# A hybrid attention and Hyena layer on one core: merge inputs read during the last inverse, m kept on chip, first tail weights split in the merge stage

## What is computed

```python
h = _rmsnorm(x, norm1_g) * (1.0 + scale1) + shift1
proj = h @ w_in
...
z = x1 * _fftconv(v, hf[:, 0], hy_bias[0])
return x2 * _fftconv(z, hf[:, 1], hy_bias[1])          # o_hy
...
g_attn, g_hy = jnp.split(jax.nn.sigmoid(gates), 2, axis=-1)
merged = g_attn * (o_attn @ w_br_attn) + g_hy * (o_hy @ w_br_hy)
x = x + gate1 * (merged @ w_out)
h2 = _rmsnorm(x, norm2_g) * (1.0 + scale2) + shift2
x = x + gate2 * (jnp.square(jax.nn.relu(h2 @ w_up)) @ w_down)
```

## Time and profile before

| | |
|---|---|
| Time, median of 3 runs | 2893.49 us (2892.32, 2893.49, 2897.98) |
| The profiled execution's own time | 2890.1 us |
| Its span | 2888.3 us |
| TensorE busy | 2707.6 us, 94% |
| VectorE, ScalarE, GpSimd busy | 44%, 31%, 28% |
| Mean granted TensorE clock | 0.961 of full speed |

### The profile page before, as it was taken

The page is one execution under the profiler, slowest core; times in us unless marked ns, Lnnn a source line. Parts: engine busy times, 40 slices in busy tenths (PEclk is TensorE's granted clock), DMA queues, the critical chain, the costliest instruction groups (busy, mean ns, idle before and its releaser), DMA issues. The chain is left out here.

```text
span 2888.3 us, 36192 instructions
## 1 busy us (share of the span) xinstructions
PE 2707.6 (94%) x14803; PEld 2318.0 (80%) x14803; DVE 1273.6 (44%) x1882; ACT 895.7 (31%) x1500; POOL 803.8 (28%) x551
## 2 busy tenths in 40 slices
PE   9687999999999999999898699798999999999998
PEld 7566887788888898888677588587888888888886
DVE  7566664445565445444876511326211212212215
ACT  2342221045555455554211421214122121121121
POOL 3546984111001010100233033213232232232230
PEclk9778999999999999999999799899999999999999
DMA  6666775442213221311756432501111111111101
GB/s 199 215 209 235 227 229 194 146 155 94 95 54 114 101 95 53 110 70 69 250 187 226 179 115 113 213 30 37 37 37 37 38 43 37 37 37 37 44 23 73
DMA packets 101858, 324.75 MB, mean 112 GB/s; under 512 B 12337, under 2 KB 30355, under 8 KB 101310
## 3 DMA queue, kind: packets, MB, share of 16 engines
q1 hardware_dynamic: 75678, 230.68, 23.2%
q0 software_dynamic: 26016, 91.76, 9.4%
HBM read 237.99 MB, written 76.02 MB: 109 GB/s over the span
## 5 line engine op out<-in xcount | busy, mean ns | idle before, releaser
L89 PE MATMUL tl_b<-tl_hi,tl_whi 128*128 128x512 f32 (+1 forms) x960 | 344.9, 359 | 21.2 <-DVE tl_lo L2447 15.3
L90 PE MATMUL tl_b<-tl_lo,tl_whi 128*128 128x512 f32 (+1 forms) x960 | 342.6, 357 | 0.0
L91 PE MATMUL tl_b<-tl_hi,tl_wlo 128*128 128x512 f32 (+1 forms) x960 | 341.7, 356 | 0.0
L2388 DVE SCALAR_TENSOR_TENSOR tl_x<-tl_b,all_mod,tl_x 128x512 f32<-128x512 f32 (+1 forms) x216 | 142.5, 661 | 375.1 <-PE tl_b L91 362.8
L2282 POOL TENSOR_TENSOR tl_wlo<-tl_raw,tl_whi 128x1024 fp32r<-128x1024 f32 x72 | 178.3, 2478 | 445.5 <-ACT tl_whi L2201 445.5
L89 PE MATMUL tl_b<-tl_uhi,tl_whi 128*128 128x512 f32 (+1 forms) x768 | 275.1, 358 | 3.5 <-POOL tl_ulo L2292 3.5
L91 PE MATMUL tl_b<-tl_uhi,tl_wlo 128*128 128x512 f32 (+1 forms) x768 | 276.6, 360 | 0.0
L89 PE MATMUL at_out<-h_hi,at_whi 128*128 128x424 f32 (+1 forms) x672 | 263.9, 393 | 12.8 <-POOL at_wlo L510 10.9
L90 PE MATMUL tl_b<-tl_ulo,tl_whi 128*128 128x512 f32 (+1 forms) x768 | 274.5, 357 | 0.0
L695 DVE TENSOR_REDUCE at_nmax<-at_s 128x1 f32<-128x1280 f32 (+1 forms) x160 | 196.8, 1272 | 111.9 <-PE at_s L562 111.3
L510 POOL TENSOR_TENSOR at_wlo<-at_raw,at_whi 128x1024 fp32r<-128x1024 f32 x28 | 66.2, 2363 | 626.5 <-ACT at_whi L611 626.5
(11 more groups left out here) (295 smaller groups left out, 5777.3 us busy)
## 6 DMA issues: line engine op xcount, KB each, us to landing
tl_raw<-in_w_tail SPq DMA_DIRECT2D x72, 512.0 KB, 3.7
hy_tab<-in_hy_tab POOLq DMA_DIRECT2D x68, 512.0 KB, 4.9
hd_wa<-in_w_adaT SPq DMA_DIRECT2D x32, 512.0 KB, 4.3
at_raw<-in_w_proj SPq DMA_DIRECT2D x28, 512.0 KB, 4.6
fd_in<-in_xT SPq DMA_DIRECT2D x16, 640.0 KB, 4.6
s_gatesT<-at_pad SPq DMA_DIRECT2D x16, 640.0 KB, 2.9
mg_gate<-s_gatesT SPq DMA_DIRECT2D x16, 640.0 KB, 5.0
fd_in<-in_w_ada SPq DMA_DIRECT2D x16, 512.0 KB, 4.0
```

What stands on the lines that cost most here:

```text
L89: pe.matmul(out, w_hi, x_hi, start=first, stop=False)
L90: pe.matmul(out, w_hi, x_lo, start=False, stop=False)
L91: return pe.matmul(out, w_lo, x_hi, start=False, stop=last)
L2388: dve.scalar_tensor_tensor(out=x1[:, n, at:at + m], in0=bank[x % GEMM_BANKS][:, 0:m], scalar=g.mod[:, gate, SEG_OF[c]:SEG_OF[c] + 1], in1= ...
```

## The change

The loads of x2 and of the first four heads of o move from the start of the merge stage into the Hyena stage, behind its last forward product, into the room of `e_hi` to `o_lo` (`early_at`). In the merge's first loop ScalarE now scales all ten units of heads 0 and 1, two behind each of the ten blocks, where ScalarE and VectorE had five each of every head behind the loop. GpSimd writes m into eight rows on chip (`m_row`), in places that are free by then; the stores, the loads and the DRAM tensor are gone. The tail's weight unit 0 is loaded, rounded and subtracted during the last merge unit. The tail reads `m_row` directly, and its x1 load follows the one of weight unit 1.

```diff
@@ stage_hyena
+        x2 = st.over("x2", early_at, [P, CHT, T])
+        o_first = st.over("o0", early_at + 4 * CHT * T, [P, ON_Z * UNITS, VD])
...
+            sp.wait_ge(runs, RUNS + FWD_RUNS)
+            sp.dma_start(x2[:], g.convT[2 * CHT:].rearrange("c p t -> p c t")).then_inc(early_in, 16)
+            for h in range(ON_Z):
+                sp.dma_start(o_first[:, h * UNITS:(h + 1) * UNITS], g.o[h]).then_inc(early_in, 16)
+            sp.wait_ge(early_in, 16 * (1 + ON_Z))
@@ stage_merge, sync
-            x2_from = g.convT[2 * CHT:].rearrange("c p t -> p c t")
-            for s, cols in enumerate((slice(CTX, T), slice(0, CTX))):
-                sp.dma_start(x2[:, :, cols], x2_from[:, :, cols]).then_inc(x_in[s], 16)
-            load_head(0)
             load_w(0, 0)
-            for h in range(1, ON_Z):
-                load_head(h)
...
-                sp.wait_ge(summed, NC * (n + 1))
-                sp.dma_start(g.mT[n], gate[s][:, 0]).then_inc(stored[s], 16)
                 if n + 2 < KD:
-                    sp.wait_ge(stored[s], 16 * (n // 2 + 1))
+                    sp.wait_ge(summed, NC * (n + 1))
                     load_gates(n + 2, s)
-            for s in range(2):
-                sp.wait_ge(stored[s], 16 * KD // 2)
+            sp.wait_ge(mm, NC * (KD - 1))
+            sp.dma_start(next_raw[:], g.d["w_tail"][0]).then_inc(next_in, 16)
@@ stage_merge, scalar
                 act.activation(o_hi[:, 0:CHT, block_columns(n)], oh[n % OH][:], ACT.Copy).then_inc(oh_h, 1)
-            act.wait_ge(small, 4)
-            scale_units(0)
+                if n == 0:
+                    act.wait_ge(small, 4)
+                for r in range(n * ALL_ACT, (n + 1) * ALL_ACT):
+                    ins = scale_unit(r // UNITS, r % UNITS)
+                    if r % UNITS == UNITS - 1:
+                        ins.then_inc(scaled_act, 1)
             weights(0)
             for h in range(HEADS):
-                if h + 1 < HEADS:
+                if ALL_ACT <= h + 1 < HEADS:
                     scale_units(h + 1)
                 upper(h)
...
+            act.wait_ge(next_in, 16)
+            act.activation(next_hi[:], next_raw[:], ACT.Copy).then_inc(next_split, 1)
@@ stage_merge, gpsimd
-                    pool.tensor_tensor(gt[:, 0, at:at + m], gt[:, 0, at:at + m], gt[:, 1, at:at + m], ALU.add
+                    if c == 0 and n in (KD - 3, KD - 2):
+                        pool.wait_ge(lo_done, n + 2)
+                    elif c == 0 and n == KD - 1:
+                        pool.wait_ge(summed, NC * n)
+                    pool.tensor_tensor(m_row[n][:, at:at + m], gt[:, 0, at:at + m], gt[:, 1, at:at + m], ALU.add
                                        ).then_inc(summed, 1)
+                    if (n, c) == (KD - 1, 1):
+                        pool.wait_ge(next_split, 1)
+                        pool.tensor_tensor(next_lo[:], next_raw[:], next_hi[:], ALU.subtract)
@@ stage_tail, sync and scalar
-            load(0)
-            for k in range(KD):
-                if k >= RAW:
-                    sp.wait_ge(m_l, k - RAW + 1)
-                sp.dma_start(m_raw[k % RAW][:], g.mT[k]).then_inc(m_in[k % RAW], 16)
-                if k == RAW - 1:
-                    load(1)
+            load(1)
             sp.dma_start(x1[:], g.d["xT"].rearrange("k p t -> p k t")).then_inc(x_in, 16)
...
-            weights(0)
             for k in range(KD):
-                act.wait_ge(m_in[k % RAW], 16 * (k // RAW + 1))
-                act.activation(hi[:, k], m_raw[k % RAW][:], ACT.Copy).then_inc(m_h, 1)
-                if k == RAW - 1:
+                act.activation(hi[:, k], m_row[k][:], ACT.Copy).then_inc(m_h, 1)
+                if k == KD // 2:
                     weights(1)
+            act.wait_ge(m_l, KD)
```

More of the change, by code:

```diff
@@ L1844, in stage_merge @@
         gate = [st.over(f"gate{s}", first_at + s * 8 * T, [P, 2, T]) for s in range(2)]
+        m_at = [z_at + 4 * T * k for k in range(4)] + [oh_at, raw0_at, x2_at, first_at]
+        m_row = [st.over(f"m{k}", at, [P, T]) for k, at in enumerate(m_at)]
+        next_at = raw0_at + 4 * T
+        next_hi, next_lo = (st.over(f"next{x}", next_at + i * 4 * KD * P, [P, KD, P], F32R) for i, x in
+                            enumerate(("hi", "lo")))
+        next_raw = st.over("nextraw", next_at + 8 * KD * P, [P, KD, P])
+        assert next_at + 12 * KD * P <= oh_at
         e2, var, std, scale = (st.sb(n, [P, N]) for n in ("e2", "var", "std", "scale"))
@@ L1848, in stage_merge @@
         oh_bank = bank[0] + bank[1][:1]
-        raw_in, gate_in, stored = ([st.sem(f"{n}{s}") for s in range(2)] for n in ("raw_in", "gate_in", "stored"))
-        o_in = [st.sem(f"o_in{h}") for h in range(HEADS)]
-        x_in = [st.sem(f"x_in{s}") for s in range(2)]
+        raw_in, gate_in = ([st.sem(f"{n}{s}") for s in range(2)] for n in ("raw_in", "gate_in"))
+        next_in, next_split = st.sem("next_in"), st.sem("next_split")
+        o_in = [st.sem(f"o_in{h}") for h in range(ON_Z, HEADS)]
         hi_done, lo_done, sig, mm, gated, summed = (
@@ L2130, in stage_tail, with weight_tile @@
     with stage(nc, "tl") as st:
+        def weight_tile(name, dt=F32R):
+            return st.sb(name, [P, KD, P], dt)
+        u_at = st.place()
+        assert u_at == from_at
+        u_hi, u_lo = (st.sb(x, [P, GT, T], F32R) for x in ("uhi", "ulo"))
+        r = [st.sb(f"r{s}", [P, 512]) for s in range(2)]
+        var, std, rstd = (st.sb(x, [P, 2, TT]) for x in ("var", "std", "rstd"))
+        st.sb("spare", [P, (rows_to - st.place()) // 4])
         x1 = st.sb("x1", [P, KD, T])
@@ L2133, in stage_tail @@
         hi, lo = (st.sb(x, [P, KD, T], F32R) for x in ("hi", "lo"))
-        raw = [st.sb(f"raw{s}", [P, KD, P]) for s in range(2)]
-        w_hi = [st.sb(f"whi{s}", [P, KD, P], F32R) for s in range(W_SLOTS)]
-        w_lo = [st.sb(f"wlo{s}", [P, KD, P], F32R) for s in range(W_SLOTS)]
-        r = [st.sb(f"r{s}", [P, 512]) for s in range(2)]
+        raw = [next_raw, weight_tile("raw1", F32)]
+        w_hi1, w_lo1, w_hi2, w_hi3 = (weight_tile(n) for n in ("whi1", "wlo1", "whi2", "whi3"))
+        assert st.place() == next_at
+        st.sb("next", [P, 3 * KD * P])
+        w_lo2, w_lo3 = (weight_tile(n) for n in ("wlo2", "wlo3"))
+        w_hi, w_lo = [next_hi, w_hi1, w_hi2, w_hi3], [next_lo, w_lo1, w_lo2, w_lo3]
         a = st.sb("a", [P, KD, 2])
-        var, std, rstd = (st.sb(x, [P, 2, TT]) for x in ("var", "std", "rstd"))
-        u_at = st.place()
-        u_hi, u_lo = (st.sb(x, [P, GT, T], F32R) for x in ("uhi", "ulo"))
         row = 4 * T
-        m_raw = [st.over(f"mraw{s}", u_at + s * row, [P, T]) for s in range(RAW)]
         sq = [st.over("sq", u_at, [P, 2, T]), st.over("fsq", hi_at, [P, 2, T])]
@@ L2151, in stage_tail @@
         raw_in = [st.sem(f"raw_in{s}") for s in range(2)]
-        m_in = [st.sem(f"m_in{s}") for s in range(RAW)]
         x_in, hi_done, lo_done, m_h, m_l, mm, added, relu, squared, u_h, u_l, a_done = (st.sem(x) for x in (
@@ L2318, in job @@
                 kind, unit, n, c = JOBS[x]
-                pe.wait_ge(lo_done, unit + 1)
+                pe.wait_ge(lo_done, unit)
                 free(x)
```

79 lines of the change are left out of this document (40 added, 39 removed).

## The result

| | before | after |
|---|---|---|
| Time, median | 2892.9 us (4 runs) | 2864.8 us (2869.85, 2855.16, 2866.71, 2862.89) |
| Ratio | | 0.9898, 95% interval 0.9882 to 0.9914 |
| The profiled execution, span | 2890.1 us, 2888.3 us | 2869.85 us, 2868.0 us |

The change makes the kernel faster by 1.0%: 28.1 us between the medians, 29.5 by the ratio. Two single executions of the study stand far apart (7756.1 us of the kernel before, 3843.49 us of the one with 672 bytes of padding); they are in the medians given and left out of the ratios.

A forecast was written before the change was run, and what follows sets the result against it. TensorE, busy 94% of the span, was taken as the bound, so its waits were counted: -7.9 - 8.7 - 7.6 + 1.3 = -22.9 us, from 2893.5 to 2870.6 us, range 2866 to 2874 (61%), wider 2865 to 2881.

The forecast's parts named there:

- Part 1: Head of the merge stage: no wait for x2, two groups of units off ScalarE's path, loop 1.1 longer; 7.9 us gained.
- Part 2: End of merge to tail: m stays on chip, so the path is barrier, rounding, split, product; 8.7 us gained.
- Part 3: Tail's first jobs: the residual lands before job 4 needs it, so 5.90 us of wait and the restart go; 7.6 us.
- the slow restart: Tail, after the gap at job 4: eight products took 3.52 us against 1.84 at full clock; 1.7 us to be gained.
- Part 4: Last inverse: the early loads share the DMA with a critical table, so TensorE resumes 1.3 us later.
- even halves: Last inverse: assumed that the two DMA queues share evenly, so the table's 0.5 MB take 2.6 us instead of 1.3.
- the upper bound of the forecast: Last inverse: all 5.24 MB of early loads served first, spectrum up to 13.0 us late; as a rival 16%, 2874 to 2882.3.
- they only write elsewhere: End of the merge: GpSimd's sums for m were taken to cost the same as before.
- more than forecast: Rival, 3%: a shorter restart at the tail's start and no cost of the early loads; 2864 to 2866 us.
- the clock did not stay low: Rival "slower", 3%: TensorE's clock could stay low through merge unit 0 after the earlier start; 2899 us and up.
- the residual landed at 1840.2: Rival, 8%: the residual still makes job 4 wait in the tail; 2878.2 if all is lost, else about 2873 to 2875.
- the twenty units did not pace the loop: Rival, 7%: the units pace the merge's first loop, 1.4 us a turn instead of 1.2, losing 2 us; 2872.6.

## Why the prediction was right, and where it was wrong

**Part 1 was right**: -7.9 forecast, -8.2 by stretch. The 6.2 us of the wait for x2 went, the two groups of units went (2.9), and the loop grew by 0.57 us, not by the 1.1 that I took. I had read VectorE's pace wrongly: 1.15 us a turn was the mean over a loop whose first two blocks come 0.6 apart, and the even pace is 1.20, in both kernels. ScalarE's 1.10 to 1.12 in its first turns fit into that, so only the two units of the last turn lengthen the loop. Undoing the twenty units cost 2.35 us, and undoing the early loads 7.1 by the profile: 5.5 for x2 (the first multiplication came 8.03 us behind the barrier and not 2.53), and 1.7 more because ScalarE's first turn then waited for head 0.

**Part 2 was right**: -8.7 forecast, -9.4 measured. From ScalarE's start on the first row to the product it took 2.85 us (it was 3.40), which is most of the difference; the barrier took the rest.

**Part 3 was right**: the wait of 5.9 us and the slow restart of 1.7 are gone, and the residual landed after 16.3 us (estimated 17). Holding the load back brought both back, the restart at the same 1.7. The row of -8.0 is near -7.6 partly by luck. From the tail's first product to job 4 it was 25.03 us and became 19.71, only 5.3 less, since the first products ran at a granted clock of 0.50 for longer (6.2 us against 4.6); and 1.0 us fell away behind job 4, most of it at a wait of the norm (3.4 us where it was 4.2), which I had not forecast. In the repeated kernel after, the first stretch is 18.28 (3.1 us at 0.50) and nothing falls away behind.

**Part 4 was right in kind and too small**: 1.3 forecast, 3.3 measured. The burst ended about where I had put it: SyncE's packets thin out from 1571.5 on, and its last data moved at 1574.68, which is 1563.2 counted as before (the last forward product came at 1554.90, 11.45 us later than in the earlier trace rows), against the 1559 to 1563 of the forecast. The step that was mis-sized is "even halves". The table had no packet moved for 3.8 us behind its issue, 2.6 us more than before, and shared only from then on, which cost the other half microsecond. Nor was the sharing even: in half microseconds from 1571.5, 13 packets of the table against 30 of SyncE's, then 21 against 27, 37 against 14, 49 against 12. The Trainium skill (DMA: Bandwidth & Descriptors, Queues, rings and completion order) has the engines go round the queues with work packet by packet. The trace shows no even halves; it doesn't refute the rule either, since a packet of the Trainium skill is a group of descriptors, and the profile's are single pieces of 4 or 5 KB.

A rival stands that the prediction did not name: service in the order of issue. The spectrum and the two tables that GpSimd had issued at 1553.86 and 1554.38, ahead of the burst, came in time; the critical table, issued behind it, got its first packet when 95% of the burst had moved. If the 16 engines finish such a queue one after another, the packets change over by degrees, as they do here. Late descriptors of the table would look alike. No run here tells these apart. What was not seen is the upper bound of the forecast, with all 5.24 MB ahead of the spectrum as well.

**The step that failed is a term that the sum does not have.** Of the moved rows I wrote "they only write elsewhere", and I costed the new layout of the tail at nothing. I never looked at the addresses. Between the first and the last DOWN product there are 848 us in which the diff changes only where things lie, and there it gained 8.9 us, since u_hi and u_lo came to lie a multiple of 256 bytes from the weights. With it the sum would have been -31.8 and the forecast 2861.7; the median measured is 3.1 us above that. The rival "more than forecast" named a shorter restart and a free part 4. The restart at the tail's start was 0.6 us longer in the profile after and 0.9 shorter in its repeat, and part 4 was not free. Its 2864 to 2866 also lie further below 2870.6 than the 1.3 us of part 4 and a restart of 1.7 can give. So its 3% and the range's low end of 2865 were too tight for want of the missing term.

None of the other rivals came true. The merge's products took 181.63 us where they took 182.03, so the clock did not stay low; the residual landed at 1840.2, 5 us ahead of its need; and the twenty units did not pace the loop.

## What to carry to other kernels

Where a diff allocates tiles anew, compare the time of a product in a stretch that the diff leaves alone before adding up its waits: 2.4% less for each product of 512 columns there was worth 8.9 us, as much as each of the three parts that were aimed at. Lay float32 operands of 512 columns so that moving and stationary tiles are a multiple of 256 bytes apart; in the kernel before, 160 bytes of padding gave nearly a third of this whole change (ratio 0.9970). Take the number for the sum from the trace before, too: the even pace of a loop, not its mean. A load moved ahead of a critical table has its price, 3.3 us here, and by the profile waiting for that table first takes it away.

## What the runs showed of the hardware that I had not expected

A 512-column float32 product takes 227 to 228 ns where the distance between its moving operand and the weight tiles is a multiple of 256 bytes, and 233 to 234 ns at remainders of 32, 96, 128 and 160, at full granted clock and with no gap between products. The 256-column products take 120.0 ns where it is a multiple of 256, and 116.7 to 119.3 where it is not. Remainders of 64, 192 and 224 were not tried. The weights of one product are loaded while the one before still streams, so the two reads may collide; no run here shows that that is the mechanism. The Trainium skill (SBUF — State Buffer, A bandwidth-pool intuition that's wrong (but worth ruling out)) gives TensorE a second, independent read port for the weights. Read as it stands, the distance should not matter; in the ten layouts measured here it does.
